# Constant multiplications left out of the waits of TensorE in the routing and ahead of the band

## What is computed

```python
for i in range(2):                                       # D = 1024, 256 tokens
    ml = silu(c) @ mod_w[i] + mod_b[i]                   # sh1, sc1, g1, sh2, sc2, g2
    hl = xl * (1.0 + sc1) + sh1
    yl = diff_attention(...) if i == 0 else pool_mixer(hl, pool_w, pool_scale)
    xl = layer_norm(ALPHA * xl + (1.0 + g1) * yl, ...)
    tokens = xl * (1.0 + sc2) + sh2
    probs = softmax(tokens @ router_w + router_b).reshape(T, 4, 4)
    g = argmax(top_k(probs, 2)[0].sum(-1))               # the group of a token
    vals, idx = top_k(probs[g], 2)                       # its two experts
    y2 = sum over the two experts e, by vals / vals.sum():
             (silu(tokens @ wg[e]) * (tokens @ wu[e])) @ wd[e]
    xl = layer_norm(ALPHA * xl + (1.0 + g2) * y2, ...)

def pool_mixer(h, w, scale):                             # four groups, windows 2, 4, 8, 16
    pooled = windowed mean over the tokens - h
    return (pooled @ w[group]) * scale
```

## Time and profile before

| | us |
|---|---|
| median of 3 runs (1342.55 to 1343.44) | 1343.26 |
| the profiled execution | 1339.71 |
| its span, first to last instruction | 1337.9 |
| TensorE busy | 1212.6 (91%) |
| VectorE busy | 411.4 (31%) |
| ScalarE busy | 163.8 (12%) |
| the fills, L654, 64 records | 31.4 |
| mean granted TensorE clock | 0.966 |
| chain of waits: L701, the expert matmuls | 44% |
| chain of waits: transfers of weights of the experts, `moe_wu` and `moe_wd` | 7% and 3% |

### The profile page before, as it was taken

The page is one execution under the profiler, slowest core; times in us unless marked ns, Lnnn a source line. Parts: engine busy times, 40 slices in busy tenths (PEclk is TensorE's granted clock), DMA queues, the critical chain, the costliest instruction groups (busy, mean ns, idle before and its releaser), DMA issues.

```text
span 1337.9 us, 12456 instructions
## 1 busy us (share of the span) xinstructions
PE 1212.6 (91%) x5055; PEld 464.8 (35%) x5055; DVE 411.4 (31%) x814; ACT 163.8 (12%) x343; POOL 18.0 (1%) x24
## 2 busy tenths in 40 slices
PE   5999999879999999999988898799999999999983
PEld 1444344444333333333323234433333333333321
DVE  1486998855301110011012115611110011002104
ACT  0200123431100100101000001110010011000000
POOL 0011010000000000000000000000000000000000
PEclk9799999998899999999997899899999999999997
DMA  9678967609699999999999996289999999999992
GB/s 330 261 261 322 336 226 251 237 32 377 281 429 426 429 429 427 430 429 428 429 428 428 389 422 254 95 347 429 426 428 429 428 429 429 428 429 429 425 428 102
DMA packets 55883, 480.66 MB, mean 359 GB/s; under 512 B 5106, under 2 KB 6530, under 8 KB 31268
## 3 DMA queue, kind: packets, MB, share of 16 engines
q1 hardware_dynamic: 42472, 433.53, 77.4%
q0 software_dynamic: 10560, 41.94, 8.5%
q10 hardware_dynamic: 2812, 4.64, 1.1%
HBM read 479.05 MB, written 1.05 MB: 359 GB/s over the span
## 4 chain that ended last, share of the span: by engine, by line
PE 71%; DMA 14%; DVE 10%; ACT 3%; issue 1%; SPq 0%; DVEq 0%; ACTq 0%
PE ps L701 44%; DMA ring<-in_moe_wu 7%; PE ps L546 5%; DMA ring<-in_mod_w 4%; PE ps L709 4%; PE ps L692 4%; DVE modp L1079 3%; DMA ring<-in_moe_wd 3%; PE ps L465 3%; PE ps L611 2%; PE ps L477 2%; PE ps L458 1%; ACT tra L988 1%; ACT work L986 1%; PE ps L575 1%
## 5 line engine op out<-in xcount | busy, mean ns | idle before, releaser
L701 PE MATMUL ps<-ring,work 128*64 128x512 f32 x3072 | 682.6, 600 | 30.7 <-ACT work L986 20.5
L701 PEld LDWEIGHTS ps<-ring,work 128*64 128x64 f32 x3072 | 216.1, 138 | 471.9 <-issue 427.9
L1347 DVE TENSOR_TENSOR work<-ps,tra 128x512 f32<-128x512 f32 x32 | 22.1, 692 | 495.5 <-ACT tra L980 495.5
L546 PE MATMUL ps<-ring 128*128 128x512 f32 x320 | 141.6, 596 | 0.7 <-ACT ring L862 0.7
L1079 DVE SCALAR_TENSOR_TENSOR modp<-ring,cs,modp 128x512 f32<-128x512 f32 x140 | 105.3, 752 | 5.0
L546 PEld LDWEIGHTS ps<-ring 128*128 128x128 f32 x320 | 59.3, 190 | 77.2 <-issue 76.2
L709 PE MATMUL ps<-tra 64*128 64x512 f32 x256 | 63.6, 615 | 21.9 <-ACT tra L988 21.9
L1350 DVE TENSOR_TENSOR work<-work,ps 128x512 f32<-128x512 f32 x32 | 22.0, 687 | 184.3 <-PE ps L701 184.3
L692 PE MATMUL ps<-h,tra 128*64 128x512 f32 x256 | 62.1, 606 | 2.2 <-DVE tra L1257 2.2
L980 ACT ACTIVATE tra<-ps 128x512 f32<-128x512 f32 x32 | 19.1, 597 | 310.2 <-PE ps L701 310.2
L988 ACT COPY tra<-ps 128x512 f32<-128x512 f32 x32 | 18.8, 587 | 249.5 <-PE ps L701 249.5
(11 more groups left out here) (163 smaller groups left out, 684.6 us busy)
## 6 DMA issues: line engine op xcount, KB each, us to landing
ring<-in_moe_wg SPq DMA_DIRECT2D x64, 2048.0 KB, 21.4
ring<-in_moe_wu SPq DMA_DIRECT2D x64, 2048.0 KB, 20.7
ring<-in_moe_wd SPq DMA_DIRECT2D x64, 2048.0 KB, 23.6
ring<-in_mod_w POOLq DMA_DIRECT2D x20, 2048.0 KB, 9.4
ring<-in_attn_wqkv SPq DMA_DIRECT2D x6, 2048.0 KB, 13.8
ring<-in_mod_w SPq DMA_DIRECT2D x4, 2048.0 KB, 18.8
ring<-in_attn_wo SPq DMA_DIRECT2D x2, 2048.0 KB, 8.9
ln<-in_ln_g ACTq DMA_DIRECT2D x4, 512.0 KB, 3.9
```

Source lines behind the costliest of these rows:

```text
L546: last = mm(bank(g % 2), hT[:, k, t * P:t * P + P], w[:, k, :], start=(k == 0), stop=(k == KT - 1))
L701: last = mm(ps[SLOTS * h:SLOTS * h + SLOTS, b, :], lhs(k0 + k), w[:, k, h * NB:(h + 1) * NB], start=(k0 + k == 0), stop=(k0 + k == KT - 1) ...
L1347: v_.tensor_tensor(hmid, bank(4), sig, ALU.mult).then_inc(sem("silu_ready"), 1)
```

## The change

The helper `keep_clock` and its three calls are taken out. Nothing else is changed, and no result depends on what is taken out. In all 32 multiplications go: 4 + 5 in each layer and 14 ahead of the band.

```diff
-            def keep_clock(bk, n):
-
-                for _ in range(n):
-                    mm(bank(bk), ident, cst[:, 0:NB], start=True, stop=True, skip_group_check=True)
-
             def route(layer):
 
                 for part in range(2 * TT):
                     t, b = part // 2, part % 2
-                    if part == 2:
-                        keep_clock(ROUTE[2], 4)
                     pe.wait_ge(sem("tokens_ready"), 2 * TT * layer + t + 1)
...
                 last.then_inc(sem("logits_done"), 1)
-                keep_clock(7, 5)
                 pe.wait_ge(sem("sel_ready"), layer + 1)
...
                     bd = w[:, 2048:4096].rearrange("p (k g n) -> p k g n", k=TT, g=4)
-                    keep_clock(4, 14)
                     pe.wait_ge(sem("tokens_ready"), 2 * TT)
```

## The result

| | before | changed kernel |
|---|---|---|
| first comparison: median, us | 1342.63 (1339.65 to 1343.44) | 1354.75 (1349.84 to 1356.94) |
| ratio, 95% interval | | 1.0084 [1.0065, 1.0103] |
| second comparison (r2): median, us | 1342.41 (1336.73 to 1348.21) | 1351.77 (1348.34 to 1355.19) |
| ratio, 95% interval | | 1.0063 [1.0037, 1.0089] |
| the profiled executions, span | 1337.9 | 1355.1 |

The median of the first lies 0.75 us above the end of the range, that of the second inside it. The two intervals overlap between 1.0065 and 1.0089.

What follows compares the result with a forecast made beforehand. In the expert loops the weight stream bounds, so delays before each layer's first unit is used up count. Layer 0 +1.4, band +0.3, layer 1 +4.5 sum to +6.2 us: 1349.5 us, 0.46% slower, range 1345.0 to 1354.0.

Steps and rivals of the forecast that it cites:

- band (last scatter to first turn): Band's matmuls ahead of layer 1's routing: half-speed stretch may last longer without fill, +0.3 us, between -0.2 and +1.6.
- The bound and the direction: Expert loops: weight stream slower than arithmetic, so a later first unit shifts the rest; slower by over 0.2%, chance 0.80.
- Rival B: Expert loop: the weight stream takes up the routing's delay, leaving 1343.3 us; chance 0.05.
- The mechanism: Routing: without fills TensorE idles and its clock is at half, so turn, router, summing and counting matmuls take longer.
- Rivals A and D: A: the fill was only in the way, 1342.3 us, chance 0.10; D: router's matmuls lift clock, +1 to +2.7 us, 0.05.
- layer 0's sum: Layer 0's routing up to the first unit used: +1.4 us in all, from -0.3 to +4.8.
- the two effects cancel: Layer 0: selection ready 1.0 us later, but 0.95 us of hold disappears, so counting begins 0.05 us later.
- hold of 0.95 us: Layer 0: the fill after the logits delays the counting behind the ready selection; removing it gives this back.
- The step from the gather to the first unit: Path to SyncE's first issue taken as 10.2 us in both layers: layer 0 +0, layer 1 +1.2 from 9.0.
- Rival C: Half speed lasts into the first unit of both layers: 8.4 us in all, 1351.7 us; chance 0.30.
- the rule on transposes: Trainium skill: transposes do not count as clock-gate activity like matmuls, so turns behind the gather would not lift the clock.

Runs made afterwards that it cites:

- r2: The changed kernel (all fills out), unchanged, measured again: 1351.77 us, ratio 1.0063 against the kernel before.
- r1: The kernel before, unchanged, measured and profiled again: 1342.05 us, ratio 0.9994.
- second pair: The repeated traces of both kernels, r1 (before) and r2 (changed): spans 1339.8 and 1352.0 us.
- r9: Kernel before with all fills, VectorE's stream norm moved ahead of the routing and ScalarE's norm-vector loads moved into the selection: 1337.32 us, ratio 0.9965.
- r10: r9 with the enlarged fills of r5, without the one between the opening of the accumulators and the gather: 1341.16 us, ratio 0.9991.
- r12: r9 once more, the same kernel: 1338.47 us, ratio 0.9978.
- r3: Kernel before without the 14 fill multiplications ahead of the band, routing fills kept: 1344.89 us, ratio 1.0018.
- r5: Kernel before with more fill between the turns, ahead of layer 1's first turn, ahead of the gather and ahead of the band: 1339.74 us, ratio 0.9986.
- r4: Kernel before without the four fills of the two routings, band fill kept: 1349.88 us, ratio 1.0063.
- r7: Changed kernel with the two norm vectors fetched at the first expert's start cut to 4 of 1024 columns: 1347.92 us, ratio 1.0035 against the kernel before.
- r6: Kernel before with each fill multiplication replaced by seven transposes of 128 columns: 1345.19 us, ratio 1.0017.

## Why the prediction came out as it did

| step of the prediction | forecast, us | changed less the first trace of before | changed (both traces) less r1 |
|---|---|---|---|
| layer 0: second turn to router | +0.7 | +0.8 | +0.8 |
| layer 0: router to sum | +0.3 | +0.3 | +0.9 |
| layer 0: sum, selection, hold, to the counting | -0.95 | -1.0 | +0.4 |
| layer 0: counting and opening, to the gather | +1.3 | +1.3 | +1.2 |
| layer 0: gather to first issue | 0 | -0.7 | +0.1 |
| band (last scatter to first turn) | +0.3 | +0.5 | +0.6 |
| layer 1: second turn to router | +0.7 | +0.8 | +0.8 |
| layer 1: router to sum | +0.9 | +0.9 | +0.9 |
| layer 1: sum to the counting | +0.4 | +0.4 | +0.4 |
| layer 1: counting and opening, to the gather | +1.3 | +1.2 | +1.2 |
| layer 1: gather to first issue | +1.2 | +0.5 | +0.4 |
| sum | +6.2 | +5.2 | +7.7 |

**The bound and the direction were right.** A delay of the first unit of a layer went through to the end: the stretches behind the first issues are no shorter without the fills (466.6 with and 466.3 without in the second pair; behind layer 1, r9, r10 and r12 aside, 463.6 to 465.4 with some or all fills, 464.8 to 465.3 without any). Rival B is out.

**The mechanism was right, and its prices came from the right rows.** The turn at 1.97 us (1.94 in the earlier trace rows), the router at 1.93 (estimate 1.95), 1.03 for the sum, counting and opening 0.10 us more a record. Rivals A and D are out: in every trace without the routing's fills the clock read 0.50 to 0.51 from the second turn to the end of the gather, the router's matmuls included.

**The step that failed is layer 0's sum, "the two effects cancel".** It took the hold of 0.95 us and the half-speed router of one profiled execution for what the fill does in layer 0. Against that execution the first four steps of layer 0 came out as forecast (third column). But in r1, r3 and r5 there is neither. The removal has nothing to give back there, and the cost is +3.5 where the forecast had +1.4. Which of the two an execution gets was not in the code: both occur in layer 0 with the fills of before (r1 and r3; before and r12). The trace itself had the hint: the same code stood in layer 1 with the clock at full. Where a state differs between two places with the same instructions, both ends belong in the sum.

**The step from the gather to the first unit was too dear, by 0.7 to 0.8 us in each layer.** The prediction took layer 0's 10.2 us for both; with the gather at half (3.56 to 3.68 us), the clock was back for the turns behind it or before the first unit, in both layers in every trace of the changed kernel, of r4 and of r7, and the path was 9.4 to 9.8 us. In layer 0 it shows only against the first trace (third column), since r1's own path was 9.4. Rival C, half speed into the first unit, did not happen in the changed kernel. It isn't impossible: beside the first trace of before it did in layer 1 of r6, in layer 0 of r9 and r10 and in both layers of r12. Its support by the rule on transposes fell with r6.

**The rest of the difference** between 6.2 and the 11.3 us of the first comparison is not in the fills: with more runs the figure is 8.5, and the places of the edits account for 7.8 of it. That the remainder is chance, above all of the clock in the lead-in, is the likeliest reading, not shown. The 0.8 us that layer 1 had too much make up for part of the 2.1 that layer 0 had too little; to that extent the nearness of 6.2 is luck.

## What to carry to other kernels

In this kernel, matmuls that compute nothing pay where the engine would idle ahead of narrow work on the path to the moment that restarts a saturated stream; what they buy is read from the short rows behind them, one fill at a time. Size them by the idle time at full speed and end them before the next real instruction can start, since at half speed, or when they start late, they hold what they were meant to help. And before a cost is taken from one profile, profile the same kernel again: here the same instructions gave a routing of 27.6 and of 30.3 us, and the same fills kept the router at full speed in seven routings of ten.

## What was not expected of the hardware

- With identical instructions the lead-in ended between 313.9 and 322.9 us, with 17 to 41 us of it at half clock after the first rise; the timed runs of the kernel before spread from 1336.7 to 1348.2 us.
- A fill did not always carry the clock through the narrow work behind it: in layer 1 of r5, behind five multiplications, the ten records of 16 columns ran at full, the clock fell in the eight of 2 columns (1.46 us for 1.05), and the multiplication right behind them took 2.05 us for the 0.9 of full speed.
- With nothing but transposes on TensorE from 862.1 us on, the clock rose from half to full at 865.4 (r6, float32).
- 1 MB of norm vectors beside the weight stream cost 1.4 to 1.8 us at the stream's restart (r7). With the vectors fetched while the ring was full the same length was 2.4 to 2.9 us shorter (r9, r10, r12), but there VectorE's operations had moved too.
- TensorE once began a fill 5.5 us late with nothing in the profile that it waited for (r4). That stays open.
